# Attention with a difference of two softmaxes: the difference formed before the transposes, VectorE scaling and GpSimd adding in six tiles of eight

## What is computed

```python
def one(args):
    a, b = args
    s1 = jnp.einsum('bqhd,bkhd->bhqk', a, k1).astype(jnp.float32) * scale
    s2 = jnp.einsum('bqhd,bkhd->bhqk', b, k2).astype(jnp.float32) * scale
    p = jax.nn.softmax(s1, axis=-1) - lam * jax.nn.softmax(s2, axis=-1)
    return jnp.einsum('bhqk,bkhd->bqhd', p.astype(v.dtype), v)
```

## Time and profile before

| what | value |
|---|---|
| median of three executions | 3094.26 us (3091.19 to 3096.95) |
| span of the profiled execution, first to last instruction | 3096.6 us |
| own time of the profiled execution | not on the page; the nearest of the three executions is 3096.95 us, 0.35 above the span |
| TensorE busy | 2979.3 us, 96% of the span |
| VectorE, ScalarE, GpSimd busy | 52%, 39%, 35% |
| granted TensorE clock, mean | 0.987 |

### The profile page before, as it was taken

The page is one execution under the profiler, slowest core; times in us unless marked ns, Lnnn a source line. Parts: engine busy times, 40 slices in busy tenths (PEclk is TensorE's granted clock), DMA queues, the critical chain, the costliest instruction groups (busy, mean ns, idle before and its releaser), DMA issues.

```text
span 3096.6 us, 49989 instructions
## 1 busy us (share of the span) xinstructions
PE 2979.3 (96%) x18212; PEld 2588.5 (84%) x18212; DVE 1608.3 (52%) x3091; ACT 1197.9 (39%) x2181; POOL 1083.4 (35%) x702
## 2 busy tenths in 40 slices
PE   7999998999999999999999999999999999999989
PEld 6689866778888888888999888987997989988877
DVE  3899738342222332313038378971114958878861
ACT  3311264342222221313124356761323647666740
POOL 2223020432222235662235334335322454332235
PEclk9999998999999999999999999999999999999999
DMA  4123331431111113342296343405336762221223
GB/s 143 59 99 128 103 81 25 137 116 48 47 47 47 50 51 128 123 144 89 92 223 208 109 120 82 119 21 175 115 109 218 215 160 82 79 72 41 88 83 128
DMA packets 224247, 325.70 MB, mean 105 GB/s; under 512 B 81414, under 2 KB 167302, under 8 KB 221910
## 3 DMA queue, kind: packets, MB, share of 16 engines
q1 hardware_dynamic: 188934, 277.29, 30.0%
q10 hardware_dynamic: 33360, 39.98, 3.8%
q0 software_dynamic: 1792, 6.29, 0.7%
HBM read 229.95 MB, written 93.57 MB: 104 GB/s over the span
## 4 chain that ended last, share of the span: by engine, by line
PE 72%; DVE 8%; issue 2%; ACT 1%; POOL 1%; DMA 1%; SPq 0%; DVEq 0%; POOLq 0%; ACTq 0%; PEldq 0%
PE psum L2280 16%; PE psum L530 13%; PE psum L2061 8%; PE psum L2483 8%; PE psum L1110 6%; PE psum L1079 6%; PE psum L1090 5%; DVE arena L2891 3%; PE psum L794 2%; PE psum L772 2%; PE psum L783 1%; DVE arena L2880 1%; PE psum L1127 1%; PE psum L3250 1%; DVE above_mixer L853 1%
## 5 line engine op out<-in xcount | busy, mean ns | idle before, releaser
L2280 PE MATMUL psum<-parts_ffn 128*128 128x512 f32 x2112 | 482.2, 391 | 3.8 <-DVE parts_ffn L2237 3.8
L2280 PEld LDWEIGHTS psum<-parts_ffn 128*128 128x128 f32 x2112 | 398.4, 189 | 87.2 <-issue 2.2
L530 PE MATMUL psum<-parts_even,parts_ffn 128*128 128x256 f32 x2496 | 304.8, 285 | 2.8 <-DVE parts_ffn L2624 1.6
L530 PEld LDWEIGHTS psum<-parts_even,parts_ffn 128*128 128x128 f32 x2496 | 302.6, 193 | 3.3 <-DVE parts_ffn L2624 2.0
L2350 DVE SCALAR_TENSOR_TENSOR arena<-psum,arena 128x1023 f32<-128x1023 f32 x88 | 112.9, 1283 | 328.2 <-ACT arena L2334 321.9
L530 PE MATMUL psum<-parts_odd 128*128 128x248 f32 x2304 | 269.2, 279 | 2.7 <-DVE parts_odd L2237 1.8
L530 PEld LDWEIGHTS psum<-parts_odd 128*128 128x128 f32 x2304 | 267.0, 189 | 3.8 <-DVE parts_odd L2237 2.0
L576 ACT ACTIVATE arena<-psum 128x256 f32<-128x256 f32 (+2 forms) x240 | 87.7, 376 | 395.6 <-PE psum L530 390.1
L444 PE MATMUL psum<-parts_mixer 128*128 128x512 f32 x912 | 210.7, 391 | 0.3 <-DVE parts_mixer L287 0.3
L444 PEld LDWEIGHTS psum<-parts_mixer 128*128 128x128 f32 x912 | 170.9, 188 | 35.9 <-DVE parts_mixer L287 0.5
L1153 ACT ACTIVATE both<-psum 128x512 fp32r<-128x512 f32 x256 | 140.0, 596 | 109.9 <-PE psum L1090 109.5
(11 more groups left out here) (344 smaller groups left out, 5905.1 us busy)
## 6 DMA issues: line engine op xcount, KB each, us to landing
arena<-ffn_up_b SPq DMA_DIRECT2D x44, 512.0 KB, 3.3
arena<-ffn_down_k SPq DMA_DIRECT2D x44, 512.0 KB, 3.6
arena<-x SPq DMA_DIRECT2D x8, 2048.0 KB, 8.4
arena<-w_in_e SPq DMA_DIRECT2D x13, 1024.0 KB, 6.3
e_tokens<-arena ACTq DMA_DIRECT2D x26, 512.0 KB, 3.0
x<-arena SPq DMA_DIRECT2D x24, 512.0 KB, 3.7
arena<-w_in_o SPq DMA_DIRECT2D x12, 992.0 KB, 6.6
o_tokens<-arena ACTq DMA_DIRECT2D x24, 496.0 KB, 3.1
```

The costliest lines, as they stand in the source:

```text
L530: last = pe.matmul(self.bank(t), self.hT[:, a, k, t * P:(t + 1) * P], self.weights.parts[:, self.weights.slot(s), b, k, :], start=(k, a, b ...
L2280: last = pe.matmul(self.core.psum[:, 4 * u + 2 * s + h, :], parts[:, s, a, k, :], self.hT[:, b, k, h * HALF:(h + 1) * HALF], start=(k, a, ...
```

## The change

The stage `diff` becomes a `DiffAttention` of its own with 32 tiles m (4 heads of 8). A tile has two score blocks (component 0 in banks 0 and 1, component 1 in banks 2 and 3), two maxima and two exponentials. The sum p0 + ratio * p1 with ratio = -lam * total0 / total1 is formed in SBUF before the turn, so that one set of eight transposes, one high and low, and one attend serve both. For tiles with t = m mod 8 in `BY_POOL` (six of eight) VectorE scales p1 in place (`scale`) and GpSimd adds it to p0 (`add`); for t = 3 and 7 VectorE does both in one instruction (`combine`). Everything is unrolled. Query and key parts have two sets, and GpSimd splits the next head piecewise between its adds; the first pieces of `latent` stand between the adds of the last four tiles. `o_pairs` has half the width, and `DiffCombine` loses its first instruction. `GainScales` gets three one-column instructions for a shift of the first exponent (`neg_shift`), which `DiffAttention.peak` adds in one more one-column instruction (`shifted`). The diff, cut; what is left out of `DiffAttention` (loads, `attend`, `back`, `take`, `high`, `low`, `finish`) is as in `WideAttention`:

```diff
+    def open_parts(self, pool):
+        hold(pool, self.loads_after)
+        for s in range(2):
+            pool.sem_inc(self.parted[s], 1)
+        self.started = True
...
+class DiffAttention:
+    HEADS, DQ, DV, LAG = 4, 64, 128, 8
+    BY_POOL = (0, 1, 2, 4, 5, 6)
...
+    def wait_combined(self, engine, m):
+
+        by_pool = [n % TT in self.BY_POOL for n in range(m + 1)]
+        engine.wait_ge(self.combined[by_pool[m]], by_pool.count(by_pool[m]))
...
+    def store(self, pool, i):
+        pool.wait_ge(self.finished, TT // 2 * (i + 1))
+        dst = tokens(self.out[:, i * self.DV:(i + 1) * self.DV])
+        pool.dma_start(dst, self.os_[:, i % 2]).then_inc(self.stored[i % 2], 16)
+        pool.wait_ge(self.stored[i % 2], self.stored_before[i % 2] + 16 * (i // 2 + 1))
+        pool.sem_inc(self.stage_free[i % 2], 1)
+
+    def gpsimd(self, pool):
+        hold(pool, self.loads_after + self.first_free)
+        self.part_queries(pool, 0, 0)
+        self.part_keys(pool, 0, 0)
+        hold(pool, self.rest_free)
+        self.part_queries(pool, 0, 1)
+        self.part_keys(pool, 0, 1)
+        self.part_values(pool, 0)
+        pool.wait_ge(self.v_parted, 2)
+        for m in range(self.M):
+            i, t = divmod(m, TT)
+            added = [n % TT in self.BY_POOL for n in range(m)].count(True)
+            if t == 4 and i >= 1:
+                self.store(pool, i - 1)
+            if added:
+                pool.wait_ge(self.combined[1], added)
+            if i + 1 < self.HEADS:
+                if t in (0, 2):
+                    self.part_queries(pool, i + 1, t // 2)
+                    pool.wait_ge(self.parted[t // 2], 4 * (i + 1) + 2)
+                if t in (1, 3):
+                    self.part_keys(pool, i + 1, t // 2)
+                    pool.wait_ge(self.parted[t // 2], 4 * (i + 1) + 4)
+                if t == 6:
+                    self.part_values(pool, i + 1)
+                    pool.wait_ge(self.v_parted, 2 * (i + 1) + 2)
+            elif t in (4, 5, 6, 7):
+                self.ahead[t - 4](pool)
+                hold(pool, self.ahead_done[t - 4])
+            if t in self.BY_POOL:
+                self.add(pool, m)
+        self.store(pool, self.HEADS - 1)
...
+    def scores(self, pe, m, c):
+        (i, t), u = divmod(m, TT), 2 * m + c
+        if t == 0:
+            pe.wait_ge(self.parted[c], 4 * i + 4)
+        if u >= 2:
+            pe.wait_ge(self.expd, u - 1)
...
+    def turn(self, pe, m):
+        self.wait_combined(pe, m)
+        for h in range(2):
+            if m:
...
+    def tensor(self, pe):
+        M = self.M
+        hold(pe, self.pe_after)
+        self.scores(pe, 0, 0)
+        for m in range(M + self.LAG):
+            if 0 <= m - 2 < M:
+                self.turn(pe, m - 2)
+            if m < M:
+                self.scores(pe, m, 1)
+            g, h = divmod(m - 4, 2)
+            if 0 <= g < M // 2:
+                self.attend(pe, g, h)
+            if m + 1 < M:
+                self.scores(pe, m + 1, 0)
+            if h == 0 and 0 <= g - 1 < M // 2:
+                self.back(pe, g - 1)
+
+    def exps(self, act, m, c):
+        if c == 0:
+            act.wait_ge(self.shifted, m + 1)
+            if m >= 2:
+                act.wait_ge(self.turned, 2 * (m - 2) + 2)
+            dst, bias = self.p0[:, m % 2], self.bias[:, m % 2:m % 2 + 1]
+        else:
+            act.wait_ge(self.neg_ready, m + 1)
+            if m >= 2:
+                self.wait_combined(act, m - 2)
+            at = 2 * (m % 2) + 1
+            dst, bias = self.p1[:, m % 2], self.nmax[:, at:at + 1]
+        src = self.core.psum[:, 2 * c:2 * c + 2, :].rearrange("p a b -> p (a b)")
+        act.activation(dst, src, ACT.Exp, bias=bias, accum_out=self.total[:, m % 8, c:c + 1]).then_inc(self.expd, 1)
...
+    def weigh(self, dve, m):
+
+        dve.wait_ge(self.expd, 2 * m + 2)
+        dve.reciprocal(self.inv[:, m % 8], self.total[:, m % 8]).then_inc(self.inverted, 1)
+        dve.wait_ge(self.inverted, m + 1)
+        if m >= 2:
+            self.wait_combined(dve, m - 2)
+        dve.tensor_scalar(self.ratio[:, m % 2:m % 2 + 1], self.total[:, m % 8, 0:1], self.inv[:, m % 8, 1:2], self.neg_lam,
+                          ALU.mult, ALU.mult).then_inc(self.ratio_ready, 1)
+
+    def scale(self, dve, m):
+
+        dve.wait_ge(self.ratio_ready, m + 1)
+        dve.tensor_scalar(self.p1[:, m % 2], self.p1[:, m % 2], self.ratio[:, m % 2:m % 2 + 1], None, ALU.mult).then_inc(self.weighed, 1)
+
+    def add(self, pool, m):
+
+        pool.wait_ge(self.weighed, [n % TT in self.BY_POOL for n in range(m + 1)].count(True))
+        pool.tensor_tensor(self.p0[:, m % 2], self.p1[:, m % 2], self.p0[:, m % 2], ALU.add).then_inc(self.combined[1], 1)
+
+    def combine(self, dve, m):
+
+        dve.wait_ge(self.ratio_ready, m + 1)
+        dve.scalar_tensor_tensor(out=self.p0[:, m % 2], in0=self.p1[:, m % 2], scalar=self.ratio[:, m % 2:m % 2 + 1],
+                                    in1=self.p0[:, m % 2], op0=ALU.mult, op1=ALU.add).then_inc(self.combined[0], 1)
...
+    def vector(self, dve):
+        for m in range(M + self.LAG):
+            if m < M:
+                self.peak(dve, m, 0)
+            for h in range(2):
+                if 0 <= m - 2 < M:
+                    self.low(dve, m - 2, h)
+            if m < M:
+                self.peak(dve, m, 1)
+            if 0 <= m - 1 < M:
+                self.weigh(dve, m - 1)
+                if (m - 1) % TT in self.BY_POOL:
+                    self.scale(dve, m - 1)
+                else:
+                    self.combine(dve, m - 1)
+            if m % 2 and 0 <= m - 7 < M:
+                self.finish(dve, (m - 7) // 2)
...
-        self.xs = core.take(TT, 2 * self.DV)
+    def __init__(self, core, name, src, gain, out_sb, after):
+        self.core, self.src, self.gain, self.out_sb, self.after = core, src, gain, out_sb, after
+        self.xs = core.take(TT, self.DV)
...
-        link(dve.scalar_tensor_tensor(out=self.first(), in0=self.second(), scalar=self.neg_lam, in1=self.first(),
-                                      op0=ALU.mult, op1=ALU.add))
...
+        diff = add(DiffAttention(core, "diff", dd[0:512], dd[512:1024], o_tok[:, 1440:1952], pairs, scales.neg_lam, scales.neg_shift,
+                                 prep.done + rest.weights.raw_free() + rest.stored_blocks(2) + gone.done, st.multiplied[:1], st.multiplied,
+                                 prep.done + rest.taken_out + gone.done,
+                                 prep.done + rest.weights.raw_free() + st.multiplied + gone.done, own, there, shared))
...
-        diff.ahead = latent.start_gpsimd
+
+        def latent_scores(s):
+            def piece(pool):
+                if s == 0:
+                    latent.open_parts(pool)
+                    hold(pool, diff.even_set_free)
+                latent.part_scores(pool, 0, s)
+            return piece
+
+        diff.ahead = [latent_scores(0), lambda pool: latent.part_values(pool, 0, 0),
+                      latent_scores(1), lambda pool: latent.part_values(pool, 0, 1)]
+        diff.ahead_done = [[(latent.parted[s], count)] for s in range(2) for count in (5, 7)]
```

186 lines of the change are left out of this document (171 added, 15 removed).

## The result

| | before | changed |
|---|---|---|
| median of four executions | 3092.80 us (3091.19 to 3096.95) | 3146.17 us (3144.42 to 3148.35) |
| span of the profiled execution | 3096.6 us | 3145.8 us |
| granted TensorE clock, mean | 0.987 | 0.973 |

The ratio is 1.0169, 95% interval 1.0154 to 1.0183: slower by 1.7%. Forecast were 3149 us, 3122 to 3172.

The account below looks back on a forecast made before the run. The prediction took `diff` to be bound by TensorE before, and by a circle of waits through all engines after the change. Its terms, 4.8 + 34 + 10.4 - 0.5 - 8 + 14 = +55 us, gave 3149 us, range 3122 to 3172.

Parts of the forecast that it names:

- Links: `diff`, 31 steps from one tile's transposes (turn) to the next: 210.8 us against 206.0, +4.8 us.
- add link: `diff`, turn to turn for a tile that GpSimd adds, the add paid in full: 7.28 us, 23 of them.
- combine link: `diff`, turn to turn for t = 3 and 7, where VectorE combines in one instruction: 5.42 us, 8 of them.
- Clock: `diff`: TensorE, standing about 2.9 us a tile, drops its clock; 1.2 us in half the tiles, +14 us (0 to 29).
- Stalls: `diff`: stores, latent loads and parts queued ahead of adds on GpSimd hold them: +34 us, bounds 29 and 38.
- Stores: Ahead of the adds of tiles 12, 20, 28, GpSimd waits for `finish` and the landing: 6.0 us each, 18 in all.
- Tile 28: Behind the store, loads of `latent` (6.5 us) and query and key parts (7.3 us) precede the add: 13.8 us.
- Start: Start of `diff`: first turn waits for the first add, near 2542.9 against 2532.47: +10.4 us, bounds 6 and 12.
- End: After the last turn, one attend less, -0.5 us; in `latent` a VectorE instruction gone four times, -8 us (5 to 11).
- The hidden add: Rival, `diff`: GpSimd's add overlaps other work of its tile and VectorE sets the pace: 3086 us, chance 0.05.
- Short stalls: Rival: store landings or `latent` loads do not hold adds, 34 us less: 3115 us, chance 0.06; clock also up, 3101, 0.03.
- Contention: Rival, `diff`: GpSimd's splitting runs into VectorE's scaling, 10 us if late in 16 tiles: 3159 us, chance 0.1.

Follow-up runs that it names:

- e12: Changed kernel with adds kept, stores, latent loads and parts moved from the adds' front, take first, 14 idle transposes before each add wait: 3105.13 us, ratio 1.0022.
- e6: Changed kernel with only the stores' place on GpSimd moved: issued at tile 5, waited for at tile 7 of the next head; ratio 1.0100 to the kernel before.
- e11: e10 with the scaling of the result (finish) done by ScalarE in two activations instead of VectorE; ratio 0.9885 to the kernel before.
- e8: Changed kernel with GpSimd adding only the first 512 of 1,024 columns of each of the 24 tiles; ratio 1.0088 to the kernel before.
- e5: Changed kernel without GpSimd adds (VectorE combines all 32 tiles) and with take at the front of an iteration; ratio 0.9901 to the kernel before.
- e10: e5 with GpSimd starting a step of parts only when VectorE has combined the tile before; ratio 0.9898 to the kernel before.

## Why the prediction was right

**Links, +4.8 forecast; the clean ones give +10.** The add link was forecast at 7.28 and is 7.45 to 7.49: 273 ns for the ratio where 0.20 from start to start was taken, 754 for the scaling (0.68 forecast), 2338 for the add (2.39), and 0.20 for the two hand-overs, for whose 0.13 the forecast named no row. The combine link was forecast at 5.42 and, free of the clock and of take, is 5.50 (e12). So 23 x 7.47 + 8 x 5.50 = 215.8, +9.8. What the forecast missed is the wait for take, 0.4 us in every second iteration: it has slack in add tiles and shows in combine tiles, 3 us.

**Clock, +14 forecast, about +14 measured.** Not half of the tiles: nine add links of 8.3 to 8.7 us, 1.1 each over 7.47, make 10, and the combine links have some 0.5 each (6.44 in the mean, 5.50 with take and clock mended, 0.4 of it take), 4. That combine tiles pay as well was not foreseen, and fewer add tiles paid than the twelve that were taken; that the two deviations cancelled is luck.

**Stalls, +34 forecast, +32 measured, by another division.** Stores were forecast at 6.0 and are 4.9 and 5.1. Tile 28 was to be 6.0 + 13.8 = 19.8 and is 19.2, but e6 shows that 16.4 of it go with the store, for its wait for `finish` keeps the loads' release back while they could have flown under other tiles. The sum was right; the reading of each part as a price of its own was not, and the order of the two waits is what kept that from showing. Tile 30: 2.4 forecast, 2.6 measured.

9.8 + 3 + 14 + 32 = 59, the 59.0 of the table.

**Start, +10.4 forecast, +10.3 measured.** The steps came as forecast, counted from the cast: the first splitting at 35.0 us (forecast 35.6), the second component's parts done at 49.0 (50.0), the first add done at 59.9 (60.0). No run took it apart; without adds, in e11, 8.3 us of it are left. **End:** forecast -0.5 and -8, measured -11.2. From the last turn to the first scores of `latent` it grew by 0.4 us (7.40 to 7.79), where -0.5 was forecast; from there on it is -11.6, of which some 6.3 are shown.

Together the terms behind the cast are +58.1 in the two profiles, where +55 were forecast. The medians differ by 53.4. The profiles' own difference is 49.2, since the stages ahead ran 8.9 us earlier in one of them. That the medians come within 2 us of the forecast +55 is thus closer than the terms deserve.

**The rivals.** The hidden add: no; e8 shows it on the path. Short stalls: no. Contention: one scaling in the changed kernel was caught, that of tile 30, 1.23 us in place of 0.75. GpSimd's splitting starts behind the last add, and kept clear of the other scalings. The mechanism is real, and it had its price where the adds were taken out, 7 us (e5 against e10).

## What to carry to other kernels

Before an operation is divided between two engines, add up the circle through all engines from one tile to the next. If nothing else of the loop can run between, the second engine's whole time is added to each tile, however idle it was: here 0.75 + 2.34 in place of 1.28 us, and +2 us a tile. An engine that is newly on the path must not have a store's landing or a load's release ahead of its work, and the price of such a wait is what it keeps back, not its own length. Where VectorE reads two SBUF tensors, put GpSimd's instructions right behind it, not beside it.
